# The second layer's input product made in two: values by token, queries and keys pair by pair and already turned

## The chip, the cores and the metric

The kernel runs on one core of a Trainium2 chip, as one launch. The metric is the device time of a launch in microseconds. Its engines are TensorE (PE: matmuls and turns, with PEld for the weight loads), VectorE (DVE), ScalarE (ACT), GpSimd (POOL) and SyncE (SP, which here only issues loads and the final stores); 16 DMA engines carry the transfers.

## What is computed

256 tokens of width 1,024 in float32 go through a two-layer transformer and then a third, wider block. What matters here is the mixer of the second layer:

```python
CD_SPLITS = (FOX_HEADS * HEAD_DIM,) * 3 + (FOX_HEADS,) + (CK_HEADS * HEAD_DIM,) * 3
CD_MIX = (FOX_HEADS + CK_HEADS) * HEAD_DIM
...
def _mixer_cd(h, w_in, b_forget, rel_bias, w_out):
    B, S, _ = h.shape
    proj = jnp.einsum('bsd,df->bsf', h, w_in)
    q_f, k_f, v_f, f_logit, q_c, k_c, v_c = _split_cols(proj, CD_SPLITS)
    o_c = _forgetting_attention(q_f.reshape(B, S, FOX_HEADS, HEAD_DIM), k_f.reshape(B, S, FOX_HEADS, HEAD_DIM),
                                v_f.reshape(B, S, FOX_HEADS, HEAD_DIM), f_logit, b_forget)
    o_d = _chunk_relpos_attention(q_c.reshape(B, S, CK_HEADS, HEAD_DIM), k_c.reshape(B, S, CK_HEADS, HEAD_DIM),
                                  v_c.reshape(B, S, CK_HEADS, HEAD_DIM), rel_bias)
    o = jnp.concatenate([o_c.reshape(B, S, -1), o_d.reshape(B, S, -1)], -1)
    return jnp.einsum('bsf,fd->bsd', o, w_out)
```

Both attentions have 8 heads of width 64. Their logits get a table added (a decay that depends on `f_logit`, or a bias by distance), then softmax, then the product with the values. `w_in` has 3,080 columns: 8 forget logits and 16 heads x (query, key, value) x 64.

## The kernel before

Weights come in chunks of up to 128 x 1,024: SyncE loads a chunk into one of four `stage` buffers (`load_chunk`), ScalarE casts it to the high half (`split_hi`, L1022), VectorE subtracts to get the low half (`split_lo`, L1326), and TensorE uses both. Four pairs of halves (`base_hi`, `base_lo`) go round, and four more (`extra_...`) at the changes between layers. The semaphores `staged`, `hi_done`, `lo_done` and `chunk_used` carry this chain; a stage buffer is free when its chunk's low half is made.

**A product by token** (`gemm`, `step`). The weights' columns are cut into steps; a step sums over 8 blocks of 128 rows. For each block and each of two token tiles of 128, the activations (`xt_hi`, `xt_lo`: turned, 128 rows of width by 256 tokens) are what is loaded into the array, and the weights stream through it: L564 (high, high), L566 (high, low), L569 (low, high). The sums, 128 tokens x n columns, lie in one of two pairs of PSUM banks; ScalarE copies them out at the end of a step (L1173). The second layer's input product `cd_in` has 7 steps of 440 columns in 28 chunks of 2 row blocks; its first two steps are written in another order (`first_steps`: L701, L705, L711), since the token tiles come one after the other from the first layer's last norm. There the turned activations come from L536 (four turns of 128 x 128), ScalarE's cast L1057 and VectorE's L1366.

**Attention, beside the products.** Two heads are a pair; the second layer has pairs 8 to 15. Each pair goes through four places in the stream of chunks, listed by hand in `STAGES`: (turn, logits, turned probabilities, sums). A place is the moment after a chunk; place 0 to 27 are `cd_in`'s chunks, then those of the output product `cd_out`. On TensorE, `turn_pair` (L840) turns two tiles of queries and two of keys, `multiply_pair` (L856) makes the logits, `turn_probs` (L870) turns the probabilities and `sum_pair` (L887) multiplies them with the values. Between them VectorE copies the turned tiles to `qk_t` (L1446), adds the table and takes maxima (L1462, L1473), ScalarE takes exponentials (L1117), VectorE scales (L1485), ScalarE copies the turned probabilities (L1125) and casts the sums (L1130), VectorE makes their low half (L1491). All engines work in the order of their program, so a wait holds up what stands behind it.

**Around it.** `cd_out` (L612) uses the pairs' sums as activations; its last four row blocks are taken half by half (the tail), and pair 15's sum stands inside the tail (`in_tail`). Before `cd_in`, in the order of VectorE's program, stand the splits of its first four chunks and then the norm of the first layer's end: sum (L1540), statistics (L1520), and the normalised halves of a token tile (L1552, L1557), for which TensorE's turns (L536) wait.

## Time and profile before

| | us |
|---|---|
| median of 3 runs (935.96 to 936.83) | 936.23 |
| the profiled execution | 934.53 |
| its span | 932.8 |
| TensorE busy | 917.3 (98%) |
| VectorE busy | 582.2 (62%) |
| ScalarE busy | 481.7 (52%) |
| GpSimd busy | 33.3 (4%) |
| granted clock of TensorE, mean | 0.999 of 2.4 GHz |

Times in the rows are counted from the start of the span. A row of the timeline gives the start, the duration, and in brackets how long the engine was idle before and what released it. Matmuls overlap in the array, so that what one costs is read from the distance between two starts, not from its duration.

### The profile page before, as it was taken

What the parts mean: (1) busy time and instruction counts of PE and PEld (TensorE: products, weight loads), DVE (VectorE), ACT (ScalarE), POOL (GpSimd) and SP (SyncE); (2) the same over time, 40 slices, a digit from 0 to 9 for tenths busy, and PEclk for the clock granted to TensorE, in tenths of its full rate; (3) what the DMA queues carried; (4) which work ended last, traced back from release to release, by engine and by line L of the source; (5) the groups of instructions that cost most, each with busy time, mean ns of one, the idle gap of its engine ahead of it and who ended that gap; (6) DMA issues with size and microseconds to landing.
All of it is one profiled execution on the core that took longest, in us unless ns stands there. A gap on an engine that the chain in (4) does not pass through costs nothing.

```text
span 932.8 us, 12124 instructions
## 1 busy us (share of the span) xinstructions
PE 917.3 (98%) x4502; PEld 759.5 (81%) x4502; DVE 582.2 (62%) x960; ACT 481.7 (52%) x781; POOL 33.3 (4%) x48
## 2 busy tenths in 40 slices
PE   6999999999999999999999999999999999999997
PEld 5888878888888888887888888878888888888875
DVE  4787687555553856668755555376646666574665
ACT  4876564444442446666444444355455654644443
POOL 1100034000000001000000000000000000000000
PEclk9999999999999999999999999999999999999999
DMA  8654457755564456454755556454554465355551
GB/s 304 242 197 136 147 181 230 265 181 182 180 220 149 147 186 209 130 162 154 259 191 191 185 185 201 147 194 137 195 192 143 147 203 158 113 196 181 200 170 66
DMA packets 46760, 169.20 MB, mean 181 GB/s; under 512 B 5384, under 2 KB 5536, under 8 KB 46064
## 3 DMA queue, kind: packets, MB, share of 16 engines
q1 hardware_dynamic: 44064, 156.09, 50.5%
q0 software_dynamic: 2640, 12.35, 4.1%
q8 instruction: 37, 0.61, 0.3%
q14 instruction: 19, 0.16, 0.0%
HBM read 167.36 MB, written 1.06 MB: 181 GB/s over the span
## 4 chain that ended last, share of the span: by engine, by line
PE 93%; DVE 3%; ACT 2%; DMA 1%; issue 0%; DVEq 0%; SPq 0%; ACTq 0%
PE psum L612 19%; PE psum L564 18%; PE psum L569 18%; PE psum L566 18%; PE psum L701 3%; PE psum L705 3%; PE psum L711 3%; PE psum L856 2%; PE psum L536 2%; PE psum L887 1%; PE psum L870 1%; PE psum L753 1%; DVE base_lo L1326 1%; PE psum L783 1%; PE psum L810 1%; ACT base_hi L1022 1%
## 5 line engine op out<-in xcount | busy, mean ns | idle before, releaser
L1326 DVE TENSOR_TENSOR base_lo<-stage,base_hi 128x1024 fp32r<-128x1024 f32 (+3 forms) x223 | 262.2, 1201 | 101.9 <-ACT base_hi L1022 101.0
L1022 ACT CAST base_hi<-stage 128x1024 fp32r<-128x1024 f32 (+3 forms) x223 | 223.2, 1033 | 56.6 <-PE psum L569 35.5
L564 PE MATMUL psum<-base_hi,xt_hi 128*128 128x512 f32 (+3 forms) x528 | 208.8, 396 | 1.9 <-ACT base_hi L1022 1.6
L566 PE MATMUL psum<-base_lo,xt_hi 128*128 128x512 f32 (+3 forms) x528 | 202.2, 383 | 0.4 <-DVE base_lo L1326 0.4
L569 PE MATMUL psum<-base_hi,xt_lo 128*128 128x512 f32 (+3 forms) x528 | 202.4, 383 | 0.0
L564 PEld LDWEIGHTS psum<-base_hi,xt_hi 128*128 128x128 f32 x528 | 99.7, 189 | 21.9 <-issue 2.8
L569 PEld LDWEIGHTS psum<-base_hi,xt_lo 128*128 128x128 f32 x528 | 99.6, 189 | 18.3 <-DVE xt_lo L1366 0.4
L566 PEld LDWEIGHTS psum<-base_lo,xt_hi 128*128 128x128 f32 x528 | 99.7, 189 | 17.7 <-DVE base_lo L1326 1.1
L1326 DVE TENSOR_TENSOR extra_lo<-stage,extra_hi 128x1024 fp32r<-128x1024 f32 (+1 forms) x68 | 80.8, 1214 | 46.9 <-ACT extra_hi L1022 46.6
L1022 ACT CAST extra_hi<-stage 128x1024 fp32r<-128x1024 f32 (+1 forms) x68 | 69.0, 1045 | 43.4 <-PE psum L612 28.9
L564 PE MATMUL psum<-extra_hi,xt_hi 128*128 128x512 f32 x160 | 63.2, 395 | 0.0
L569 PE MATMUL psum<-extra_hi,xt_lo 128*128 128x512 f32 x160 | 62.4, 390 | 0.0
L566 PE MATMUL psum<-extra_lo,xt_hi 128*128 128x512 f32 x160 | 62.3, 390 | 0.0
L612 PE MATMUL psum<-base_hi,ht_hi 128*128 128x512 f32 x144 | 51.5, 400 | 0.0
L612 PE MATMUL psum<-base_lo,ht_hi 128*128 128x512 f32 x144 | 50.2, 392 | 0.7 <-DVE base_lo L1326 0.7
L612 PE MATMUL psum<-base_hi,ht_lo 128*128 128x512 f32 x144 | 50.1, 391 | 0.0
L1074 ACT CAST ht_hi<-psum 128x512 fp32r<-128x512 f32 x22 | 12.9, 587 | 65.4 <-PE psum L753 65.4
L1187 ACT ACTIVATE qk_t<-psum 128x256 f32<-128x256 f32 x44 | 14.5, 381 | 62.1 <-PE psum L569 54.0
L1373 DVE TENSOR_TENSOR ht_lo<-psum,ht_hi 128x512 fp32r<-128x512 f32 x22 | 15.2, 690 | 49.9 <-ACT ht_hi L1074 49.9
L564 PE MATMUL psum<-base_hi,ht_hi 128*128 128x512 f32 (+1 forms) x106 | 41.2, 389 | 0.0
L569 PE MATMUL psum<-base_hi,ht_lo 128*128 128x512 f32 (+1 forms) x106 | 39.4, 372 | 0.0
L566 PE MATMUL psum<-base_lo,ht_hi 128*128 128x512 f32 (+1 forms) x106 | 39.4, 372 | 0.0
(198 smaller groups left out, 1320.4 us busy)
## 6 DMA issues: line engine op xcount, KB each, us to landing
stage<-in_w_up SPq DMA_DIRECT2D x80, 512.0 KB, 4.4
stage<-in_w_down SPq DMA_DIRECT2D x44, 512.0 KB, 4.3
...
```

Source lines behind the costliest of these rows:

```text
L536: last = pe.transpose(turn_bank(name, g)[:, k * P:(k + 1) * P], src(k0 + k, t), ident[:, :])
L564: pe.matmul(acc, ah, wh, start=(k == 0), stop=False)
L566: pe.matmul(acc, ah, wl, start=False, stop=False)
L569: last = pe.matmul(acc, al, wh, start=False, stop=(k == g.kc - 1))
L612: last = pe.matmul(psum[:, 2 * ((g.u0 + half) % 2) + t, :], a, w(c, half * 512, 512), start=(k == 0 and w is w_hi and a is ah), stop=summed)
L701: pe.matmul(acc, ah, w_hi(c, at, g.n), start=(k == 0), stop=False)
L705: pe.matmul(acc, al, w_hi(c, at, g.n), start=False, stop=False)
L711: last = pe.matmul(acc, ah, w_lo(c, at, g.n), start=False, stop=(k == g.kc - 1))
L856: last = pe.matmul(psum[:, LOGIT_BANK + e, t * P:t * P + nk], qk_t[rows, b, t * P:(t + 1) * P], qk_t[rows, b, S:S + nk], start=True, stop= ...
L1022: act.copy(w_hi(c, 0, w), stage_of(c, w)).then_inc(hi_done, 1)
L1326: dve.tensor_tensor(w_lo(c, 0, w), stage_of(c, w), w_hi(c, 0, w).bitcast(F32), ALU.subtract).then_inc(lo_done, 1)
L1373: dve.tensor_tensor(ht_lo[:, at, :], turn_bank(name, g).rearrange("p (k n) -> p k n", k=2), ht_hi[:, at, :].bitcast(F32), ALU.subtract).th ...
```

## The change

The columns of `cd_in` are the same, and so is what is computed with them. They are now made by two products. `cd_v` makes the forget logits and the values, 1,032 columns, by token as before: 3 steps of 344 columns, 12 chunks of 2 row blocks. `cd_qk` then makes queries and keys in 8 steps, one for each pair. In a step the weights are loaded into the array (128 query columns or 128 key columns of the pair at a time) and the activations stream through it, so that the sums come out turned, channel by token. `xt_hi` and `xt_lo` now lie side by side in one tile `xt`, so that a high-weights matmul of 512 columns makes the products with both halves of all 256 tokens in one bank; a low-weights matmul of 256 columns adds its part to the first 256. At the end of a step ScalarE copies columns 256 to 512 of both banks to `qk_t` (`copy_lows`) and VectorE adds columns 0 to 256 (`add_lows`). The turns `turn_pair` and the copies `copy_pair` of pairs 8 to 15 are gone. A chunk of `cd_qk` has 4 row blocks of 256 columns; there are 16.

The weights lie in memory in blocks of 128 rows with all 3,080 columns, and are picked from there: a chunk of `cd_qk` in one transfer with rows of 1 KB, a chunk of `cd_v` in 3 or 4 transfers (`value_pieces`), where one transfer with rows of 3,520 bytes stood before. The table of places is adapted, and pair 15's sum stands after `cd_out`'s chunk 3.

```diff
-             ("cd_in", 8, 2, 440, 7), ("cd_out", 8, 1, 1024, 1), ("up1", 8, 2, 512, 11), ("down1", 22, 1, 1024, 1),
+             ("cd_v", 8, 2, CD_V // 3, 3), ("cd_qk", 8, 4, 256, 8), ("cd_out", 8, 1, 1024, 1), ("up1", 8, 2, 512, 11), ("down1", 22, 1, 1024, 1),
...
+def pair_block(pair, n):
+    return FOX_H + (3 * pair + n) * 2 * HD
+def value_pieces(step):
+    n = CD_V // 3
+    blocks = [(0, FOX_H, 0)] + [(FOX_H + 2 * HD * p, 2 * HD, pair_block(p, 2)) for p in range((FOX_H + CK_H) // 2)]
+    pieces = []
+    for at, width, column in blocks:
+        lo, hi = max(at, step * n), min(at + width, (step + 1) * n)
+        if lo < hi:
+            pieces.append((lo - step * n, hi - lo, column + lo - at))
+    return pieces
+def loads_of(g, n):
+    return len(value_pieces(n * g.kp // g.kc)) if g.name == "cd_v" else 1
...
-            count[s] = count.get(s, 0) + 1
+            count[s] = count.get(s, 0) + loads_of(g, n)
...
-L1_PLACES = [("cd_in", n) for n in range(28)] + [("cd_out", n) for n in range(5)]
+L1_PLACES = ([("cd_v", n) for n in range(12)] + [("cd_qk", n) for n in range(16)]
+             + [("cd_out", n) for n in range(4)])
...
-    (11, 12, 15, 16), (13, 14, 17, 18), (15, 16, 19, 20), (17, 18, 21, 22), (21, 22, 25, 26), (23, 24, 27, 28),
-    (25, 26, 28, 29), (28, 29, 31, 32)])})
+    (13, 14, 17, 18), (15, 16, 19, 20), (17, 18, 21, 22), (19, 20, 23, 24), (21, 22, 25, 26), (23, 24, 27, 28),
+    (25, 26, 29, 30), (27, 28, 30, 31)])})
...
-        xt_hi = sb("xt_hi", [P, 8, S], F32R)
-        xt_lo = sb("xt_lo", [P, 8, S], F32R)
+        xt = sb("xt", [P, 8, 2, S], F32R)
+        xt_hi, xt_lo = xt[:, :, 0, :], xt[:, :, 1, :]
...
+        def pair_sums(j):
+            u = PRODUCTS["cd_qk"].u0 + j
+            both = psum[:, 2 * (u % 2):2 * (u % 2) + 2, :]
+            return u, qk_t[:, j % 2, :].rearrange("p (b n) -> p b n", b=2), both[:, :, 0:S], both[:, :, S:2 * S]
...
+            def cd_columns(k0, count, column, width):
+                return bass.AP(tensor=d["w_cd_in"].tensor, offset=k0 * P * CD_W + column,
+                               ap=[[CD_W, P], [P * CD_W, count], [1, width]])
             def load_chunk(g, n):
                 c = g.c0 + n
                 if STAGE_LAST[c] >= 0:
                     sp.wait_ge(lo_done, STAGE_LAST[c] + 1)
-                sp.dma_start(stage_of(c, WIDTH[c]), d["w_" + g.name][n]).then_inc(staged[STAGE[c]], 16)
-            for g in GEMMS.values():
+                if g.name == "cd_qk":
+                    sp.dma_start(stage_of(c, WIDTH[c]).rearrange("p (k n) -> p k n", k=g.kp),
+                                 cd_columns(n % 2 * g.kp, g.kp, pair_block(n // 2, 0), g.n)
+                                 ).then_inc(staged[STAGE[c]], 16)
+                elif g.name == "cd_v":
+                    for at, width, column in value_pieces(n * g.kp // g.kc):
+                        sp.dma_start(stage_of(c, WIDTH[c]).rearrange("p (k n) -> p k n", k=g.kp)[:, :, at:at + width],
+                                     cd_columns(n * g.kp % g.kc, g.kp, column, width)).then_inc(staged[STAGE[c]], 16)
+                else:
+                    sp.dma_start(stage_of(c, WIDTH[c]), d["w_" + g.name][n]).then_inc(staged[STAGE[c]], 16)
...
-                                if in_tail and t == 0 and halves[0] == 0 and k == end - 3:
-                                    in_tail()
...
-                pe.wait_ge(pair_copied, p + 1)
+                if p < 8:
+                    pe.wait_ge(pair_copied, p + 1)
+                else:
+                    pe.wait_ge(*read("cd_qk", p - 7))
...
-                    turn_pair(p)
+                    if p < 8:
+                        turn_pair(p)
...
-            first_steps("cd_in", "x1", 1, {7: lambda: [heads_banks("f1"), cumulate()]})
-            gemm("cd_in", xt_hi, xt_lo, 0, None, attending("cd_in", *range(8, 28)), first=2)
+            def step_by_pair(j):
+                g = PRODUCTS["cd_qk"]
+                u = g.u0 + j
+                pe.wait_ge(acc_free[u % 2], 2 * (u // 2))
+                for m in range(2):
+                    c = g.c0 + 2 * j + m
+                    for kk in range(g.kp):
+                        k = m * g.kp + kk
+                        for high in ((True, False) if k < g.kc - 1 else (False, True)):
+                            for b in range(2):
+                                acc, at = psum[:, 2 * (u % 2) + b, :], kk * g.n + b * P
+                                if high:
+                                    pe.wait_ge(hi_done, c + 1)
+                                    last = pe.matmul(acc, w_hi(c, at, P), xt[:, k, :, :].rearrange("p a n -> p (a n)"),
+                                                     start=(k == 0), stop=(k == g.kc - 1))
+                                else:
+                                    pe.wait_ge(lo_done, c + 1)
+                                    last = pe.matmul(acc[:, 0:S], w_lo(c, at, P), xt_hi[:, k, :],
+                                                     start=False, stop=False)
+                    last.then_inc(chunk_used, 1)
+                    attend("cd_qk", 2 * j + m)
+            first_steps("cd_v", "x1", 1, {7: lambda: [heads_banks("f1"), cumulate()]})
+            gemm("cd_v", xt_hi, xt_lo, first=2)
+            for j in range(8):
+                step_by_pair(j)
             wide("cd_out", ht_hi, ht_lo, None, between=attending("cd_out", *range(4)), first_turn=first_part("f1", 2),
-                 first_pair=8, in_tail=lambda: attend("cd_out", 4))
+                 first_pair=8)
...
+            def copy_lows(j):
+                u, dst, highs, lows = pair_sums(j)
+                act.wait_ge(chunk_used, PRODUCTS["cd_qk"].c0 + 2 * j + 2)
+                act.wait_ge(pair_logits, max(8, 8 + j - 1))
+                act.copy(dst, lows).then_inc(pair_lows, 1)
+            gemm("cd_v", copy_to(lambda j, t, acc: (proj1[:, t, j * 344:(j + 1) * 344], acc[:, 0:344])),
+                 {4: log_sigmoid})
+            gemm("cd_qk", None, {**attending("cd_qk", *range(16)),
+                                 **{2 * j + 1: lambda j=j: [copy_lows(j), attend("cd_qk", 2 * j + 1)]
+                                    for j in range(8)}})
+            wide("cd_out", attending("cd_out", *range(4)), TAIL)
...
+            def add_lows(j):
+                u, dst, highs, lows = pair_sums(j)
+                dve.wait_ge(pair_lows, j + 1)
+                dve.tensor_tensor(dst, dst, highs, ALU.add).then_inc(acc_free[u % 2], TT)
+            gemm("cd_v", None, {4: forget_abs, 5: forget_log, 7: copy_cumulated})
+            gemm("cd_qk", None, {**attending("cd_qk", *range(16)),
+                                 **{2 * j + 1: lambda j=j: [add_lows(j), attend("cd_qk", 2 * j + 1)]
+                                    for j in range(8)}})
+            wide("cd_out", attending("cd_out", *range(4)), 2)
```

In the order of TensorE's program, at a turn (L840) between two chunks of `cd_in` before:

```order
L564 MATMUL psum<-base_hi,xt_hi 128x440 [waits hi_done]
L566 MATMUL psum<-base_lo,xt_hi 128x440 [waits lo_done]
L569 MATMUL psum<-base_hi,xt_lo 128x440
L840 MATMUL psum<-ident,arena 128x128 [waits pair_copied,acc_free0]
L840 MATMUL psum<-ident,arena 128x128 x3
L564 MATMUL psum<-base_hi,xt_hi 128x440 [waits hi_done]
L566 MATMUL psum<-base_lo,xt_hi 128x440 [waits lo_done]
L569 MATMUL psum<-base_hi,xt_lo 128x440
L564 MATMUL psum<-base_hi,xt_hi 128x440 [waits hi_done]
```

and in the new program, in the middle of a step of `cd_qk` (L1009 and L1013 are `step_by_pair`, L924 is `sum_pair`, L893 is `multiply_pair`, "xt" the activations):

```order
L1009 MATMUL psum<-xt,base_hi 128x512 [waits hi_done] x2
L1013 MATMUL psum<-xt,base_lo 128x256 [waits lo_done] x2
L924 MATMUL psum<-probs_t,arena 64x256 [waits pair_copied,acc_free1,o_lo,probs_copied]
L924 MATMUL psum<-probs_t,arena 64x256
L924 MATMUL psum<-probs_t,arena 64x128 x2
L893 MATMUL psum<-qk_t 128x128 [waits probs_copied,pair_max,acc_free1]
L893 MATMUL psum<-qk_t 128x128
L893 MATMUL psum<-qk_t 128x256 x2
L1009 MATMUL psum<-xt,base_hi 128x512 [waits hi_done] x2
L1013 MATMUL psum<-xt,base_lo 128x256 [waits lo_done] x2
L1009 MATMUL psum<-xt,base_hi 128x512 [waits hi_done] x2
```

No turn stands there any longer; the logits wait for the accumulator's semaphore `acc_free`, which VectorE's add raises, in place of `pair_copied`.

In the order of ScalarE's program, around the end of a step with a pair's exponentials, before (L1117 exponentials, L1173 copies of the sums, L1125 turned probabilities, L1022 high halves):

```order
L1022 CAST base_hi<-stage 128x880 [waits chunk_used,staged0]
L1117 ACTIVATE pair_probs,pair_st<-pair_probs,pair_st 128x128 [waits pair_max]
L1117 ACTIVATE pair_probs,pair_st<-pair_probs,pair_st 128x256
L1117 ACTIVATE pair_probs,pair_st<-pair_probs,pair_st 128x128
L1117 ACTIVATE pair_probs,pair_st<-pair_probs,pair_st 128x256
L1173 COPY arena<-psum 128x440 [waits chunk_used]
L1173 COPY arena<-psum 128x440
L1125 COPY probs_t<-psum 128x2x384 [waits pair_summed,probs_turned]
L1022 CAST base_hi<-stage 128x880 [waits chunk_used,staged1]
```

and in the new program (L1183, L1311, L1191 and L1088 are the same four):

```order
L1183 ACTIVATE pair_probs,pair_st<-pair_probs,pair_st 128x128 [waits pair_max]
L1183 ACTIVATE pair_probs,pair_st<-pair_probs,pair_st 128x256
L1183 ACTIVATE pair_probs,pair_st<-pair_probs,pair_st 128x128
L1183 ACTIVATE pair_probs,pair_st<-pair_probs,pair_st 128x256
L1311 COPY qk_t<-psum 128x512 [waits pair_logits,chunk_used]
L1191 COPY probs_t<-psum 128x2x384 [waits pair_summed,probs_turned]
L1088 CAST base_hi<-stage 128x1024 [waits chunk_used,staged1]
```

One copy of 128 x 512 stands where two of 128 x 440 stood, behind the exponentials again, and the logits of the step's pair now depend on it.

In the order of SyncE's program, the loads before:

```order
L422 DMA late_stage_50<-in_w_up 128x1024 x2
L422 DMA stage<-in_w_up 128x1024 [waits lo_done] x40
L422 DMA stage<-in_w_down 128x1024 [waits lo_done] x22
L422 DMA stage<-in_w_cd_in 128x880 [waits lo_done] x28
L422 DMA stage<-in_w_cd_out 128x1024 [waits lo_done] x8
L422 DMA late_stage_49<-in_w_up 128x1024 [waits lo_done,pair_max,chunk_used]
```

and in the new program, up to the second chunk of `cd_v`:

```order
L463 DMA stage<-in_w_down 128x1024 [waits lo_done] x22
L460 DMA stage<-in_w_cd_in 128x2x8 [waits lo_done]
L460 DMA stage<-in_w_cd_in 128x2x128 x2
L460 DMA stage<-in_w_cd_in 128x2x80
L460 DMA stage<-in_w_cd_in 128x2x8 [waits lo_done]
L460 DMA stage<-in_w_cd_in 128x2x128 x2
L460 DMA stage<-in_w_cd_in 128x2x80
L460 DMA stage<-in_w_cd_in 128x2x8 [waits lo_done]
```

A wait for the stage buffer stands ahead of four issues instead of one.

## Rows read from the trace of the kernel before

**Rows 1.** The page: busy time of TensorE; the two halves of the weight split

```profile
PE 917.3 (98%) x4502; PEld 759.5 (81%) x4502; DVE 582.2 (62%) x960; ACT 481.7 (52%) x781; POOL 33.3 (4%) x48
...
L1326 DVE TENSOR_TENSOR base_lo<-stage,base_hi 128x1024 fp32r<-128x1024 f32 (+3 forms) x223 | 262.2, 1201 | 101.9 <-ACT base_hi L1022 101.0
...
L1022 ACT CAST base_hi<-stage 128x1024 fp32r<-128x1024 f32 (+3 forms) x223 | 223.2, 1033 | 56.6 <-PE psum L569 35.5
```

**Rows 2.** Stretches: length, busy PE, PEld, DVE, ACT, POOL, clock, DMA share, GB/s

```profile
339.86:407.41 67.55, 67.55 (x406) 57.42 (x405) 44.87 (x127) 40.84 (x96) 4.98 (x8) 1.00 0.56 178
...
407.41:437.16 29.75, 29.10 (x156) 22.12 (x153) 21.86 (x43) 17.98 (x31) 0.00 (x0) 1.00 0.58 195
```

**Rows 3.** Who waited for whom: TensorE, 296 to 450 us

```profile
PE psum L612 <- DVE base_lo L1326: 0.7, 2, 0.5
```

**Rows 4.** Timeline, TensorE, 440 columns, with a turn: start, duration (us)

```profile
341.13 0.36 PE L566 MATMUL psum<-base_lo,xt_hi 128*128 128x440 f32 x1
...
350.33 0.36 PE L569 MATMUL psum<-base_hi,xt_lo 128*128 128x440 f32 x1
...
350.53 0.60 PE L840 MATMUL psum<-ident,arena 128*128 128x128 f32 x4
...
351.16 0.36 PE L566 MATMUL psum<-base_lo,xt_hi 128*128 128x440 f32 x1
```

**Rows 5.** Timeline, TensorE, at 256 and at 512 columns

```profile
49.24 0.28 PE L564 MATMUL psum<-base_hi,ht_hi 128*128 128x256 f32 x1
...
50.91 0.28 PE L569 MATMUL psum<-base_hi,ht_lo 128*128 128x256 f32 x1
...
428.11 0.40 PE L612 MATMUL psum<-base_hi,ht_hi 128*128 128x512 f32 x1
...
434.74 0.39 PE L612 MATMUL psum<-base_hi,ht_lo 128*128 128x512 f32 x1
```

**Rows 6.** Timeline, ScalarE: turned tile; a pair's last exponential

```profile
327.50 0.59 ACT L1057 CAST xt_hi<-psum 128x512 fp32r<-128x512 f32 x1 [3.57 <-PE psum L536]
...
371.27 0.49 ACT L1117 ACTIVATE pair_probs<-pair_probs,pair_st 128x256 f32<-128x256 f32 x1
```

**Rows 7.** Timeline, VectorE, at the first layer's last norm

```profile
310.28 1.08 DVE L1326 TENSOR_TENSOR extra_lo<-stage,extra_hi 128x880 fp32r<-128x880 f32 x1 [0.71 <-ACT extra_hi L1022]
...
313.57 0.69 DVE L1540 SCALAR_TENSOR_TENSOR x<-x,psum 128x512 f32<-128x512 f32 x1 [0.89 <-PE psum L612]
...
316.25 0.75 DVE L1557 SCALAR_TENSOR_TENSOR x<-x,ln_st,ln_par 128x512 f32<-128x512 f32 x1
...
325.68 0.75 DVE L1557 SCALAR_TENSOR_TENSOR x<-x,ln_st,ln_par 128x512 f32<-128x512 f32 x1
...
328.12 0.69 DVE L1366 TENSOR_TENSOR xt_lo<-psum,xt_hi 128x512 fp32r<-128x512 f32 x1 [1.69 <-ACT xt_hi L1057]
```

**Rows 8.** Timeline, TensorE: turns after the norm; a pair's sum and logits

```profile
317.38 0.60 PE L536 MATMUL psum<-ident,x 128*128 128x128 f32 x4
...
326.87 0.60 PE L536 MATMUL psum<-ident,x 128*128 128x128 f32 x4
...
328.09 0.60 PE L536 MATMUL psum<-ident,x 128*128 128x128 f32 x4
...
366.68 0.87 PE L887 MATMUL psum<-probs_t,arena 128*64 128x256 f32 x8
...
367.48 0.93 PE L856 MATMUL psum<-qk_t 64*128 64x128 f32 x8
```

**Rows 9.** Timeline, SyncE's queue: issues of transfers

```profile
1.24 0.42 SPq L416 DMA_DIRECT2D ident<-in_ident  x1
...
1.71 0.90 SPq L422 DMA_DIRECT2D stage<-in_w_ab_in  x2
...
300.69 0.33 SPq L422 DMA_DIRECT2D stage<-in_w_cd_in  x1
```

**Rows 10.** SyncE's issue line, 298 to 350 us

```profile
DMA to landing us min/median/max: 3.1/4.5/6.9
```

90 lines of the change are left out of this document (39 added, 51 removed).

## Prediction, on record before the changed kernel was run

> **What bounds the kernel now.** I read the page first: TensorE is busy for 98% of the span and carries 93% of the chain that ended last [rows 1]. The other engines matter only where they make TensorE wait or hand it more work. The view by stretches then says the same of the part that is changed: in the input product of the second layer (339.9 to 407.4 us) TensorE is busy for 67.55 of 67.55 us, at a granted clock of 1.00 (2.4 GHz), with the 16 DMA engines at 56%; only in the output product after it is 0.65 us missing [rows 2]. The list of waits agrees: from 296 to 450 us TensorE waited 0.7 us in all, for two low halves of weights in the tail of that output product [rows 3]. So a microsecond taken from TensorE's stream there is a microsecond of the result, unless a new wait eats it, and no waiting can be won but that 0.7 us.
>
> "Busy" hides what one matmul costs, since the bars overlap (a bar of 0.36 us, while starts are 0.20 us apart). I therefore work with the spacing of starts. At 440 columns there are 46 spacings between the starts at 341.13 and 350.33 us: 0.200 us each [rows 4]. At 256 columns 14 spacings lie between 49.24 and 50.91 us: 0.119 us. At 512 columns 29 lie between 428.11 and 434.74 us: 0.2286 us [rows 5]. Each of these matmuls loads its own weights, and the load does not show beyond this spacing, not even at 256 columns.
>
> **The change, part by part.** *The product's own matmuls.* Before: 7 steps x 8 row blocks x 2 token tiles x 3 passes = 336 of 440 columns, 147,840 columns. After: values 3 x 8 x 2 x 3 = 144 of 344 columns; queries and keys 8 steps x 8 x 2 = 128 of 512 and 128 of 256 columns: again 147,840. In time: before 336 x 0.200 = 67.2 us. For 344 columns I interpolate between 256 and 440: 0.119 + 88/184 x 0.081 = 0.158 us. After: 144 x 0.158 + 128 x 0.2286 + 128 x 0.119 = 22.7 + 29.3 + 15.3 = 67.3 us. **+0.1 us**, for 64 matmuls more.
>
> The Trainium skill speaks against this on the page "TensorE: Matmul & The Clock Gate", section "Back-to-back issue gap": in a stream of weight loads and matmuls it gives 131 ns at N=512 and 81 ns at N=128, so most of the cost belongs to the matmul and little to its columns. Drawn as a line, an estimate from that page is 122 ns at 440, 109 at 344 and 98 at 256 columns: 41.0 us before, 45.0 after, +4.0 us in place of +0.1. The measured 228.6 ns at 512 columns disagree with it, and the rows decide.
>
> *The turns of queries and keys.* Eight times TensorE turned two query and two key tiles of a pair (L840, x4). A turn costs the stream more than its start shows: the last matmul ahead of it starts at 350.33, the second behind it at 351.16, 0.83 us where two spacings are 0.40 [rows 4]. 8 x 0.43 = **-3.4 us**. What depended on them, the 0.69 us copies on VectorE, ran beside the product and gives TensorE nothing. The attention inserts themselves (logits, turned probabilities, sums) are as many as before; two of them stand together once more than they did, which saves one restart of the stream of about 0.1 us (0.28 instead of 0.20 us behind an insert, [rows 4]): **-0.1 us**.
>
> *The new link between product and logits.* Before, logits waited for one VectorE copy, issued a place ahead. Now, when a pair's step ends, ScalarE copies the low sums and VectorE adds the high ones; the logits wait for that. No such pair of instructions is in the trace; by the nearest 128x512 rows it is 0.59 us (ScalarE from PSUM) and 0.69 us (VectorE from PSUM) [rows 6, 7]. ScalarE has the previous pair's exponentials ahead of it. Logits that start at 367.48 [rows 8] have their last exponential starting at 371.27, done at 371.76 [rows 6]: 4.3 us after. In the new order the step ends 0.86 us (the logits matmuls, taken from their bar of 0.93) + one chunk of 8 x 0.2286 + 8 x 0.119 = 2.8 us after the same point, so 3.65 us: ScalarE is 0.65 us late (367.48 + 4.28 against 367.48 + 3.65), the sum is there 0.65 + 0.59 + 0.69 + 0.2 for two hand-overs = 2.1 us after the step. TensorE asks for it after the turned probabilities, another chunk (2.8) and the earlier pair's sum (0.8: its start at 366.68, the logits' at 367.48): 3.6 us without the probabilities. At least 1.5 us to spare, eight times: **0**. Bounds: 0 if the spare time holds; if each engine had its longest neighbour, a split of 1.0 and 1.2 us [rows 1], in front of it once more, 0.7 us per pair is missing, less the time of the six turned probabilities (0.4 us or more): 0.3 us, 2.4 us in all. Only at the end is it tighter: the output product's second accumulator needs the last pair's sum (2.1 us) after 6 x 0.2286 = 1.4 us and those probabilities: **+0.1**.
>
> *The entry from the first layer.* Before the second token tile's turns TensorE now has narrower work. Up to the first turn it does 36 matmuls, up to the second 40; at 0.042 us less each it arrives 1.5 and 1.7 us sooner, at 325.4 instead of 326.87 and at 326.4 instead of 328.09 [rows 8]. The norm's last write on VectorE runs from 325.68 to 326.43 [rows 7]. What was 1.7 us of cover becomes zero: I take **+0.2 us**, between 0 and 0.8.
>
> *The loads.* A values chunk comes in 3 or 4 pieces with rows of 32 to 512 bytes, where one issue with rows of 3,520 bytes stood; 44 issues for 12 chunks. A piece of 256 short rows on SyncE's queue is not in the trace. Issues there follow each other every 0.47 us (1.24 to 1.71) [rows 9], and the quickest whole chunk of 440 KB was there 3.1 us after its issue [rows 10]; a last piece of 80 KB needs no more than that, and I take 2.3 us. VectorE splits the first four of these chunks before it starts the norm of the first layer's end: before, the fourth split started at 310.28, and the norm later waited 0.89 us for TensorE until 313.57 [rows 7]. After: 16 issues from 300.69 (first row of [rows 9]), the last at 300.69 + 15 x 0.47 = 307.7, landed 310.0, cast 0.7, split 0.85: 311.6. The norm's first half (0.68 + 0.69 and the steps between, 1.4 us) ends at 313.0, before TensorE's half. **0**, with 0.5 us to spare, and 0.38 us more behind it (the norm's write ends at 317.00, TensorE's turn starts at 317.38 [rows 7, 8]). The bound above is a rival below. The pair chunks are one issue of 512 rows of 1 KB and have some 4 us of TensorE's time each: 0.
>
> *The end of the output product.* The last pair's sum now stands at a chunk's end and not inside the tail, so ScalarE is held back from the last splits less long. The 0.7 us of [rows 3] lie here, in two waits with a restart of 0.1 us each: 0.9 us. After, the last low half still comes late: ScalarE's cast of the sum (0.4 us, estimated from 0.59 for twice the width), hi split 1.0 and lo split 1.2 [rows 1], with 0.3 us of hand-overs 2.9 us after the sum, when TensorE wants it after 10 spacings of 0.2286, 2.3 us: 0.6 us, with a restart 0.7. **-0.2 us**, between 0 and -0.9.
>
> Sum: +0.1 - 3.4 - 0.1 + 0.1 + 0.2 - 0.2 = **-3.3 us**. The span is 932.8 us and the profiled execution 934.53 us with the 1.7 us around it, so 931.2; the median of the three runs is 936.23, 1.7 us above the profiled one, so **932.9 us**.
>
> **The rivals.**
> *The pieces come late.* At a pitch p between issues the fourth chunk's split ends at 311.6 + 15 (p - 0.47). From p = 0.53 TensorE waits, and each further 0.1 us costs 1.5 us; 0.6 costs 1.1 us (934.0), 0.7 costs 2.6 (935.5), 0.9 costs 5.6 (938.5, slower). A piece that lands 2 us later instead costs 1.1 us. For it: three times the issues of a shape not in the trace. Against: the pitch is that of any transfer shown, and the data need less than the DMA engines' idle half. 19%. The Trainium skill's page "DMA: Bandwidth & Descriptors", section "Specifications", has 512 B as the least transfer at line rate and says that shorter ones are read, modified and written; 20 of the 44 pieces are shorter. No row here shows it; it would make this rival likelier, which is counted in the 19%.
>
> *New waits in the pair chain or at the entry.* 0.3 us at each logits (2.4) or 0.8 at the entry: 933.7 to 935.3. For it: two engines in place of one, and no cover left at the entry. Against: the 1.5 us to spare. 11%.
>
> *The stream of alternating widths is slower (the other side).* If the weight load (0.188 us as a bar) does not fit behind a 256-column matmul when it is followed by another load, the 128 low matmuls are 0.188 instead of 0.119 us apart: +8.8 us, 941.7, slower. It decides at 26 ns per low matmul (gain gone). Against: the 256-column stretch has a load with every matmul and keeps 0.119. 5%, the page's 4 us included.
>
> *More than forecast*, if the whole tail stall goes and nothing new comes, 4.2 us in place of 3.3: 932.0 or less, 3%. The forecast itself 62%.
>
> **Numbers.** 0.2%, 1.9 us, is about what a measurement of this kernel tells from no change: faster below 934.4, slower above 938.1. The forecast's own range is 932.0 to 934.0. Faster: 62 + 3 + half of the second rival + a quarter of the first, about 71%. Same: the rest of both and the weaker end of the third, 19%. Slower: 10%. The range that leaves out 2 in 10 goes up over half of the first rival and down past the best sum: 931.5 to 936.6.
>
> **What would show it.** Right: the stretch from the first product matmul to the output product shorter by about 3.4 us beyond the entry; starts 0.229 and 0.119 us apart in the new stream; no wait of TensorE on the new VectorE add; SyncE's issues 0.47 us apart; the first layer's norm starting at the same time. Wrong: a wait for the norm's write at the first turn, a longer pitch of issues, low matmuls further apart than 0.13 us, or TensorE held at the logits by the add.

## The result, and the profile after

| | before | changed |
|---|---|---|
| median of its runs | 936.1 us (934.46 to 936.83, 4 runs) | 929.97 us (929.34 to 931.11, 4 runs) |
| ratio | | 0.9942, 95% interval 0.993 to 0.9954 |
| profiled execution, its span | 934.53, 932.8 us | 930.03, 928.3 us |

By the medians the changed kernel is 6.1 us faster, by the ratio 5.4 us (4.3 to 6.6), where 3.3 were forecast. Its time lies 1.5 us below the forecast's wider range (931.5 to 936.6 us), in the part that was given 3%. The direction and the main mechanism (the turns leave TensorE's stream) were right. One term was mis-sized, and so was the level on which the sum was set, as the rows show.

The page, and the two stretches that answer to [rows 2] (the product of values, queries and keys from its third step on; the output product with the next norm's first turns). The first of them can't be set against before's as it stands, since it holds 2,392 of the 3,080 columns here and 2,200 there; the table further down compares like with like.

```profile
PE 913.2 (98%) x4534; PEld 755.9 (81%) x4534; DVE 582.1 (63%) x960; ACT 482.5 (52%) x781; POOL 34.4 (4%) x48
```

```profile
337.39:404.66 67.27, 67.27 (x437) 56.56 (x436) 45.98 (x127) 42.85 (x97) 5.97 (x8) 1.00 0.66 197
404.66:432.75 28.09, 27.94 (x148) 21.33 (x147) 21.42 (x42) 17.34 (x28) 0.00 (x0) 1.00 0.60 207
```

TensorE is again busy all the time at a granted clock of 1.00 (2.4 GHz), and 4.1 us less of it is needed. Its waits from 296 to 450 us, against 0.7 us in [rows 3]:

```profile
PE psum L653 <- DVE base_lo L1401: 0.2, 1, 0.2
```

The timeline of TensorE in the new stream: L607 and L610 are two of the three passes at 344 columns, L1009 the 512-column matmul of queries and keys (two to a row), L1013 the 256-column one.

```profile
337.39 0.31 PE L607 MATMUL psum<-base_lo,xt 128*128 128x344 f32 x1
...
344.63 0.32 PE L610 MATMUL psum<-base_hi,xt 128*128 128x344 f32 x1
344.79 0.63 PE L1009 MATMUL psum<-xt,base_hi 128*128 128x512 f32 x2
345.26 0.40 PE L1013 MATMUL psum<-xt,base_lo 128*128 128x256 f32 x2
345.49 0.63 PE L1009 MATMUL psum<-xt,base_hi 128*128 128x512 f32 x2
```

46 spacings from 337.39 to 344.63 us are 0.157 us each; two 512-column matmuls take 0.47 us and two 256-column ones 0.23 us, 0.70 together. The forecast had 0.158 us for the first, and 2 x 0.2286 + 2 x 0.119 = 0.695 us for the others.

**Where the time went**, by starts of TensorE that both timelines have (A: second turn of the first layer's last norm, B: first matmul of the output product, C: first turn of the norm after it, D: first turn of the norm after the feed-forward, E: its last turn):

| stretch | before | after | difference | forecast |
|---|---|---|---|---|
| start to A | 319.21 | 319.57 | +0.36 | 0 |
| A to B | 88.20 | 85.09 | -3.11 | -2.8 |
| B to C | 27.56 | 26.26 | -1.30 | -0.5 |
| C to D | 187.30 | 186.94 | -0.36 | 0 |
| D to E | 12.28 | 12.20 | -0.08 | 0 |
| E to the end | 298.25 | 298.24 | 0 | 0 |

The forecast column is its own sum laid out by place. Seven of the eight turns stood between A and B, the eighth in the output product, so of -3.4 a share of -3.0 goes to A to B and -0.4 to B to C. From A to E the profiled executions differ by 4.85 us, not 3.3; about half of what is missing lies in B to C. (The second pair of profiles, runs 1 and 12, differs by 4.60: 315.05 and 310.45 us.) The +0.36 ahead of A has nothing to do with the change: 0.34 of it is there at the first layer's first norm, whose turns start at 130.45 us before and at 130.79 after.

### The profile page after: what moved, and what is told of

Same layout as the page of the kernel before. It is cut to its first block, busy times and chain, and to the rows that moved or that the text cites. A ratio compares the mean times of both kernels' runs of the same rounds, so it can differ in the third digit from the quotient of the medians.

```text
span 928.3 us, 12232 instructions
## 1 busy us (share of the span) xinstructions
PE 913.2 (98%) x4534; PEld 755.9 (81%) x4534; DVE 582.1 (63%) x960; ACT 482.5 (52%) x781; POOL 34.4 (4%) x48
## 4 chain that ended last, share of the span: by engine, by line
PE 96%; DVE 2%; ACT 2%; DMA 1%; issue 0%; SPq 0%; DVEq 0%; ACTq 0%
PE psum L653 21%; PE psum L605 17%; PE psum L610 17%; PE psum L607 17%; PE psum L1009 3%; PE psum L740 3%; PE psum L744 3%; PE psum L750 3%; PE psum L893 2%; PE psum L1013 2%; PE psum L577 1%; PE psum L924 1%; PE psum L907 1%; PE psum L792 1%; PE psum L822 1%; PE psum L849 1%
## 5 line engine op out<-in xcount | busy, mean ns | idle before, releaser
L1088 ACT CAST base_hi<-stage 128x1024 fp32r<-128x1024 f32 (+3 forms) x223 | 224.4, 1036 | 58.1 <-PE psum L610 32.7
L605 PE MATMUL psum<-base_hi,xt 128*128 128x512 f32 (+3 forms) x464 | 183.5, 395 | 2.6 <-ACT base_hi L1088 2.3
L607 PE MATMUL psum<-base_lo,xt 128*128 128x512 f32 (+3 forms) x464 | 178.3, 384 | 0.4 <-DVE base_lo L1401 0.4
L610 PE MATMUL psum<-base_hi,xt 128*128 128x512 f32 (+3 forms) x464 | 178.6, 385 | 0.0
L605 PEld LDWEIGHTS psum<-base_hi,xt 128*128 128x128 f32 x464 | 87.7, 189 | 19.4 <-ACT base_hi L1088 2.7
L610 PEld LDWEIGHTS psum<-base_hi,xt 128*128 128x128 f32 x464 | 87.6, 189 | 17.2 <-DVE xt L1441 0.4
L607 PEld LDWEIGHTS psum<-base_lo,xt 128*128 128x128 f32 x464 | 87.7, 189 | 17.1 <-DVE base_lo L1401 1.1
L1088 ACT CAST extra_hi<-stage 128x1024 fp32r<-128x1024 f32 (+1 forms) x68 | 68.4, 1037 | 47.4 <-PE psum L653 26.4
L605 PE MATMUL psum<-extra_hi,xt 128*128 128x512 f32 x160 | 63.2, 395 | 0.0
L610 PE MATMUL psum<-extra_hi,xt 128*128 128x512 f32 x160 | 62.4, 390 | 0.0
L607 PE MATMUL psum<-extra_lo,xt 128*128 128x512 f32 x160 | 62.4, 390 | 0.0
L1009 PE MATMUL psum<-xt,base_hi 128*128 128x512 f32 x128 | 41.0, 404 | 0.0
L610 PE MATMUL psum<-base_hi,ht_lo 128*128 128x512 f32 (+1 forms) x106 | 39.4, 372 | 0.0
```

The costliest lines, as they stand in the source:

```text
L605: pe.matmul(acc, ah, wh, start=(k == 0), stop=False)
L607: pe.matmul(acc, ah, wl, start=False, stop=False)
L610: last = pe.matmul(acc, al, wh, start=False, stop=(k == g.kc - 1))
L1009: last = pe.matmul(acc, w_hi(c, at, P), xt[:, k, :, :].rearrange("p a n -> p (a n)"), start=(k == 0), stop=(k == g.kc - 1))
L1088: act.copy(w_hi(c, 0, w), stage_of(c, w)).then_inc(hi_done, 1)
```

## The experiments

Times are medians. Each group ran on one chip beside its own runs of before: 935.36 us (17 runs) for the first four, 935.64 (21) for the next four, 935.66 (21) for the last four.

**1. The changed kernel again.**

> The changed kernel itself once more, on the chip of the runs beside it. Theory A (the parts add up: turns 3.4 us, the tail of the output product 0.9, the entry and the link 0, so some 4.5 to 4.9 us as in the two profiled executions): ratio 0.9950, gain 4.3 to 5.0 us. Theory B (timed executions of the kernel before carry a loss of 1 to 2 us that its profiled one does not show and that the change removes): gain 5.8 to 6.5 us, ratio 0.9935.

Measured: 930.48 us (929.80 to 930.63, 5 runs), ratio 0.9939 (0.9927 to 0.9951); profiled 930.58. With the four runs above, nine executions of the changed kernel have their median at 930.26 us. Seventeen more of before gave 935.36. By these medians the gain is 4.9 us; by the ratio it is 5.7 (4.6 to 6.8), so this run by itself does not tell theory A from theory B. All executions together give 935.65 - 930.26 = 5.4 us (run 12).

**2. Before, without the turns of pairs 8 to 15.**

```diff
             def attend(name, n):
...
-                    turn_pair(p)
+                    if p < 8:
+                        turn_pair(p)
...
-                    copy_pair(p)
+                    if p < 8:
+                        copy_pair(p)
```

> The kernel before with one part of the change alone: the eight turns of queries and keys and their copies on VectorE are left out, and the logits of pairs 8 to 15 are made from stale tiles. If a turn costs TensorE's stream 0.43 us and nothing else hangs on it: 3.4 us faster, within 0.3. Rival: the copies on VectorE or the wait for the copy held TensorE up unseen as well: 4.5 us or more faster. A third possibility, that the stream only moves its waits (the tail stays as it is): 2.5 us or less.

Measured: 933.05 us (932.01 to 935.02, 7 runs), ratio 0.9971 (0.996 to 0.9983), 2.3 us faster than before by the medians and 2.7 by the ratio. The profile says why it is not 3.4: with the turns gone, TensorE comes to pair 8's probabilities before VectorE has masked pair 9, and VectorE had waited for the decay table that GpSimd builds for pairs 8 to 11 (VectorE's and TensorE's timeline; in brackets the idle time ahead and who ended it):

```profile
356.55 0.29 DVE L1464 CUSTOM_DVE_ANT_0 pair_probs<-psum,fox_table 128x128 f32<-128x128 f32 x1 [2.83 <-POOL fox_table L504]
```

```profile
363.25 0.17 DVE L1475 TENSOR_SCALAR pair_st<-pair_st 128x4 f32<-128x4 f32 x1
```

```profile
363.52 0.84 PE L871 MATMUL psum<-ident,pair_probs 128*128 128x128 f32 x6 [1.02 <-issue]
```

The profile names no releaser for the wait of 1.02 us, but in the program TensorE waits there for pair 9's maxima, whose last instruction (L1475) ends at 363.42 us, 0.1 ahead. In the trace A to C is 2.2 us shorter than in before, and with the wait and a restart of 0.1 us that makes the turns' 3.3. The tail's two waits are still there (0.6 us), so the third possibility has the size nearly right, but for another reason. The turns alone could not have been removed from before at their full price: pair 9's maxima end at 362.42 us there and TensorE comes at 363.09, which is some 0.6 us to spare, and in this run the table came 0.9 us later by itself (13.6 us behind the store in place of 12.7).

**3. The changed kernel with eight idle turns.**

```diff
                 for p in at_stage((name, n), 0):
                     if p < 8:
                         turn_pair(p)
+                    else:
+                        for m in range(4):
+                            pe.transpose(psum[:, QK_BANK, m * P:(m + 1) * P], x[:, m % 2, m * P:(m + 1) * P],
+                                         ident[:, :])
```

> The changed kernel with eight idle turns (four transposes of 128x128 each, of other data, results unused) at the places where a pair's turn would stand. Theory: 8 x 0.43 = 3.4 us slower than the changed kernel. What is then left against the kernel before is the gain of everything but the turns: by theory A 1.2 us, by theory B 2.5 us or more.

Measured: 934.16 us (933.11 to 935.06, 10 runs), 3.7 us above run 1 on the same chip. In its trace A to B is 88.68 us, 3.59 more than after: 0.45 us for each turn, against 0.43 in the forecast. The rest of the change, without the turns' gain, is worth 1.2 us against before by the medians, 1.7 (0.8 to 2.5) by the ratio.

**4. The changed kernel with the last pair's sum back inside the tail.**

```diff
-    (25, 26, 29, 30), (27, 28, 30, 31)])})
+    (25, 26, 29, 30), (27, 28, 31, 32)])})
...
+                                if in_tail and t == 0 and halves[0] == 0 and k == end - 3:
+                                    in_tail()
```

> The changed kernel with the last pair's turned probabilities and sum put back where they stood before: the probabilities after chunk 3 of the output product, the sum inside its tail. Theory: the tail's loss comes back, TensorE waits twice for low halves there: 0.9 us slower than the changed kernel (between 0.7 and 1.2), and nothing else moves. Rival (my forecast's size for this part): 0.2 us slower.

Measured: 931.37 us (930.80 to 931.40, 5 runs), 0.9 us above run 1. B to C is 27.21 us, 0.95 more than after, with the two waits of [rows 3] back (0.6 us in all). So the place of that sum is worth 0.9 us, which the forecast had at 0.2.

**5. The kernel before without the wait for the decay table.**

```diff
-                return Head(HD, HD ** -0.5, q, k, v, fox_table[:, h, :], False, cut(o1, h * HD, HD), None, None)
+                return Head(HD, HD ** -0.5, q, k, v, table[:, h, :], False, cut(o1, h * HD, HD), None, None)
...
-                if p == 8 or p == 10:
-                    dve.wait_ge(fox_masked, 2 if p == 8 else 4)
+                if p == 8:
+                    dve.wait_ge(rel_ready, 2)
                 if p == 12:
-                    dve.wait_ge(rel_ready, 2)
+                    dve.wait_ge(fox_masked, 4)
```

> The kernel before, with one thing changed in the computation: the scores of pairs 8 to 11 get the relative-position table added in place of the decay table, so that VectorE no longer waits for GpSimd's decay table before it masks pair 8. Every instruction stays in its place; only that wait is gone. In the profiled execution of before the masking of pair 8 waits 1.95 us for the table and TensorE's copies of pair 8's probabilities then come through with some 0.6 us to spare; in the run without turns the same chain was 1.0 us late. Theory A (in many timed executions of before the table comes later still, and TensorE waits for pair 8): the median falls by 0.5 to 1.5 us against the kernel before and the spread of the executions, 3.2 us so far, shrinks to about 1.5 us. Theory B (the spread of before has another source, such as start-up or the first layer): no change within 0.3 us and the same spread.

Measured: 935.23 us (934.29 to 936.94, 11 runs), ratio 0.9994 (0.9985 to 1.0003). The spread of before is still there (2.6 us against 2.3), so the table is not its main source. The median moved by 0.4 us, inside an interval of -1.4 to +0.3: whether late tables cost the timed executions some tenths isn't decided by it.

**6 and 7. The changed kernel with a later decay table.** The change makes the values first, so the table's chain starts 3.6 us earlier (GpSimd stores its rows at 338.08 us, before at 341.63). These two runs take that back and more: the store comes 5.3 us later than in after in the first and 6.2 us in the second.

```diff
                 pool.wait_ge(cum_copied, 1)
+                pool.wait_ge(hi_done, PRODUCTS["cd_qk"].c0 + 1)
                 pool.dma_start(fox_rows, cum_k[0:FOX_H, :]).then_inc(fox_stored, 16)
```

(`+ 2` in the other.)

> The changed kernel; GpSimd stores the cumulated decay only after the high halves of the first chunk of queries and keys are written, some 4 us later than it does there and about when the kernel before does. Nothing else moves. The chain from that store to the table took 12.7 to 14.0 us in six profiles, so the table comes at about 356 us in place of 352, the masking of pair 8 ends at about 358.5, and that of pair 9, which must end before TensorE copies pair 8's probabilities at 363.6, at 363.5 to 365. Theory A (that chain is a part of the gain): 0.3 to 1.3 us slower than the changed kernel (930.5 us on the first chip), with a wait of TensorE at pair 8's probabilities in the profile and a wider spread. Theory B (the chain has time to spare in both kernels): no change within 0.3 us.

> As the run before it, with the store after the second chunk of queries and keys, some 5.9 us later than in the changed kernel. Theory A: TensorE waits 2 to 3 us at pair 8's probabilities, and the time is 2 to 3 us above the changed kernel's, that is 932.5 to 933.5 us; each further us of delay costs about a whole one. Theory B: no change, or under 0.5 us.

Measured: 931.13 us (930.65 to 931.64, 5 runs) and 934.75 us (931.84 to 937.53, 11 runs): 0.9 and 4.5 us above the nine runs of the changed kernel, which ran on other chips. Theory A's size holds for the first run and is too small for the second, and the place was wrong in both: TensorE did not wait at pair 8's probabilities but at pair 9's logits (0.5 and 3.1 us). VectorE and TensorE of the later one:

```profile
358.05 0.29 DVE L1538 CUSTOM_DVE_ANT_0 pair_probs<-psum,fox_table 128x128 f32<-128x128 f32 x1 [5.07 <-POOL fox_table L546]
```

```profile
362.66 0.93 PE L894 MATMUL psum<-qk_t 64*128 64x128 f32 x8 [3.11 <-DVE qk_t L1774]
```

The masking waits 5.07 us, pair 8's exponentials on ScalarE wait for the masking, ScalarE's copy of pair 9's low sums stands behind the exponentials in its queue, and the adding step behind the copy. So what makes one pair late makes the next pair's link late as well.

The wait is not all that the later run lost. A to B is 89.86 us, 4.77 more than in after: 3.2 lie ahead of pair 9's logits, and 1.6 behind them, where no wait is listed. There, behind the idle stretch of 3.11 us, TensorE's granted clock had fallen from 2.4 to 1.2 GHz, from 364.1 to 367.5 us. The last number but two of this row is the clock of a stretch, as a share of 2.4 GHz:

```profile
364.00:367.00 3.00, 3.00 (x12) 2.55 (x11) 2.96 (x11) 0.78 (x3) 0.00 (x0) 0.51 0.73 204
```

The timed executions fit that: the two whose mean clock was 0.999 took 931.84 and 933.10 us, the nine at 0.995 to 0.997 took 933.50 to 937.53. In the first run, with its wait of 0.5 us, the clock stayed at 1.00.

**8. A longer link between product and logits.**

```diff
+                for _ in range(3):
+                    settle(dve.tensor_copy(row_g[:, 0:512].rearrange("p (b n) -> p b n", b=2), highs))
```

> The changed kernel with three idle copies of 128x512 on VectorE ahead of each pair's adding step, each finished before the next, some 2.2 us more in the link between a pair's queries and keys and its scores, eight times. In the profile after, that add ends 2.45 us before TensorE comes to the scores of that pair. Theory A (the link is hidden with about 2.4 us to spare, as the forecast had it at no cost): no change within 0.5 us. Rival (some pairs have less to spare, or VectorE's splits of weights come late behind the longer link): a wait of 0.3 us or more for each pair, 2 us or more in all.

Measured: 944.69 us (944.02 to 944.82, 4 runs), 14 us more. I had counted spare time in the wrong place. The forecast's link in the profile after (ScalarE, VectorE, TensorE):

```profile
371.77 0.50 ACT L1183 ACTIVATE pair_probs<-pair_probs,pair_st 128x256 f32<-128x256 f32 x1
...
372.26 0.57 ACT L1311 COPY qk_t<-psum 128x512 f32<-128x512 f32 x1
```

```profile
372.93 0.69 DVE L1773 TENSOR_TENSOR qk_t<-qk_t,psum 128x512 f32<-128x512 f32 x1 [1.35 <-ACT qk_t L1311]
```

```profile
376.07 0.93 PE L893 MATMUL psum<-qk_t 64*128 64x128 f32 x8
```

The add ends at 373.62, TensorE comes at 376.07: 2.45 us to spare for this pair (2.3 to 2.6 for six of the eight, 1.3 and 1.0 for the first two). But logits, masking, exponentials, copy, add and the next pair's logits form a ring. With the three copies it takes 9.25 us from logits to logits:

```profile
371.39 0.93 PE L893 MATMUL psum<-qk_t 64*128 64x128 f32 x8 [0.75 <-DVE qk_t L1775]
```

```profile
380.64 0.93 PE L893 MATMUL psum<-qk_t 64*128 64x128 f32 x8 [0.86 <-DVE qk_t L1775]
```

Less the 2.14 us of the copies and some 0.1 us between them that is 7.0 us, where the stream gives it 8.09 (376.07 to 384.16). The ring has 1.1 us to spare, not 2.45: VectorE's scaling and its split stand behind the add, and the next masking behind them.

The ring is only a part of the 14 us. In the trace A to B is 93.00 us, 7.9 more than in after: those are the ring's losses. B to C is 32.22 us, 5.96 more. Of these, 3.07 us are one wait of the output product's second accumulator for the last pair's add, and the clock takes most of the rest. It was at 1.2 GHz from 416.6 to 423.4 us, after seven waits of up to 1.2 us and inside this last one:

```profile
417.62 0.80 PE L653 MATMUL psum<-base_hi,ht_hi 128*128 128x512 f32 x1 [3.07 <-DVE qk_t L1775]
```

```profile
417.00:423.00 6.00, 5.38 (x22) 3.53 (x22) 3.21 (x8) 0.93 (x2) 0.00 (x0) 0.50 0.31 89
```

From that matmul to the first one behind the logits (423.50) it takes 5.89 us, where the same instructions take 3.12 in after: 2.8 us for the clock.

**9. Each chunk of values loaded by one issue.**

```diff
-    return len(value_pieces(n * g.kp // g.kc)) if g.name == "cd_v" else 1
+    return 1
...
+    weights["cd_v"] = np.concatenate([cd[:, :FOX_H]] + [cd[:, pair_block(p, 2):pair_block(p, 2) + 2 * HD]
+                                                        for p in range(8)], 1)
```

> The changed kernel with the columns of the values laid out one behind the other in memory, so that each of their 12 chunks is loaded by one issue in place of 3 or 4. The computation is the same. In the profile after, the pieces are issued every 0.47 us and land in a median of 2.5 us, and TensorE does not wait for the first layer's norm that stands behind them on VectorE. Theory A (the pieces cost nothing, as forecast): no change within 0.4 us of the changed kernel. Rival (pieces with rows of 32 to 512 bytes slow other transfers, or move the norm at the entry): 0.5 to 1.5 us faster.

Measured: 930.94 us (929.78 to 931.22, 5 runs); the nine runs of the changed kernel have 930.26. That is 0.7 us more, just outside theory A's 0.4 but on the side away from the rival's gain, and against other chips; in the traces nothing differs (A to B 85.11 us, B to C 26.26, after 85.09 and 26.26). So the pieces cost the time nothing, as forecast. They do hold up the norm at the entry a little, as the rival had it: without them its write ends 0.37 us ahead of TensorE's first turn (317.07 and 317.44), with them 0.1 (317.64 and 317.73). Their group in the profile after (the first three numbers are the duration of an issue in ns), and the first 16 issues on SyncE's queue:

```profile
L460 SPq DMA_DIRECT2D stage<-in_w_cd_in x44: 368/469/1115, 301.1 to 335.8; - x44
...
DMA to landing us min/median/max: 2.0/2.5/3.8
```

```profile
301.06 8.06 SPq L460 DMA_DIRECT2D stage<-in_w_cd_in  x16
```

An issue lasts 0.469 us, but the next one starts 0.51 us after it: 8.06 us for 16, less the last one's 0.47, over 15. The forecast and the expectation above have 0.47 us as the distance.

**10. The changed kernel, last free split ahead of the last sum.**

```diff
                 if (name, n) in LAST_SUMS:
-                    split_to(min(done["due"], PRODUCTS[LAST_SUMS[name, n]].c0))
+                    end = PRODUCTS[LAST_SUMS[name, n]].c0
+                    split_to(min(ahead(end - 4), end))
```

(on ScalarE and on VectorE)

> The changed kernel; ScalarE and VectorE split the last free chunk of the output product's weights before they take up the last pair's sum, not behind it. In the profile after, the one wait for that chunk reads 0.15 us, but the starts around it (0.55 us in place of 0.23, then 0.34 in place of 0.24) make it cost 0.42 us. Theory A (a listed wait costs its length and about 0.3 us of restart): 0.4 us faster than the changed kernel, at the edge of what can be told, and no wait left in the output product. Theory B (the cost of a wait is its listed length): 0.15 us, no difference. Rival: the last sum now comes late and its own split is waited for, 0 to 0.7 us slower.

Measured: 929.08 us (928.86 to 929.69, 5 runs), ratio 0.9928 (0.9915 to 0.9942) against before, 1.2 us under the nine runs of the changed kernel on other chips and 1.9 under run 9 on the same one. Of that the trace shows 0.48: B to C is 25.78 us in place of 26.26, and TensorE has no wait from 296 to 640 us. This is the fastest version measured here.

**11. The kernel before, one split ahead of the copy of the last probabilities.**

```diff
                 for p in at_stage((name, n), 2):
+                    if p == PAIRS - 1:
+                        split_to(done["chunks"] + 1)
                     copy_probs(p)
```

> The kernel before; ScalarE splits one chunk of the output product's weights before it copies the last pair's turned probabilities, not behind that copy (it had been idle for 2.06 us there). Nothing else changes. In the profile of before the two waits for the next chunks read 0.5 and 0.2 us, while the starts around them show 1.29 us lost. Theory A (that stall is the tail's term and costs 1.3 us, of which the change saved 0.9): 0.8 to 1.3 us faster than the kernel before. Theory B (a stall costs its listed length): 0.5 to 0.7 us. Rival (the tail has nothing to do with it and the gain beyond the turns comes from the earlier layer): no change.

Measured: 933.78 us (933.17 to 936.51, 11 runs), 1.9 us under before by the medians; ratio 0.9985 (0.9976 to 0.9994), 1.4 us (0.6 to 2.2). B to C is 26.60 us in place of 27.56, 0.96 less. Theory A's 0.8 to 1.3 us is met by the trace, and by the ratio within its interval. The timeline of the tail in before, where the sum stands just ahead of the first row, and in this run:

```profile
425.32 0.50 PE L612 MATMUL psum<-base_hi,ht_hi 128*128 128x512 f32 x1
426.30 0.50 PE L612 MATMUL psum<-base_lo,ht_hi 128*128 128x512 f32 x1 [0.48 <-DVE base_lo L1326]
426.64 0.40 PE L612 MATMUL psum<-base_hi,ht_lo 128*128 128x512 f32 x1
...
427.44 0.51 PE L612 MATMUL psum<-base_lo,ht_hi 128*128 128x512 f32 x1 [0.17 <-DVE base_lo L1326]
427.78 0.49 PE L612 MATMUL psum<-base_hi,ht_lo 128*128 128x512 f32 x1
428.11 0.40 PE L612 MATMUL psum<-base_hi,ht_hi 128*128 128x512 f32 x1
```

```profile
425.69 0.50 PE L612 MATMUL psum<-base_hi,ht_hi 128*128 128x512 f32 x1
426.03 0.39 PE L612 MATMUL psum<-base_lo,ht_hi 128*128 128x512 f32 x1
...
427.35 0.39 PE L612 MATMUL psum<-base_hi,ht_hi 128*128 128x512 f32 x1
```

Six spacings behind the sum take 2.79 us in before and 1.66 here. So waits of 0.65 us in the list cost 1.1 us and more. ScalarE's idle time was there, 2.06 us ahead of its copy of the last turned probabilities:

```profile
423.24 0.80 ACT L1125 COPY probs_t<-psum 128x768 f32<-128x768 f32 x1 [2.06 <-PE psum L870]
```

**12. The kernel before again.**

> The kernel before, unchanged, for a second profiled execution of it and for the spread of its timed ones. The forecast put the changed kernel's timed executions 1.7 us above its profiled one because before's median of three was. Theory A (that distance was a draw: the three were high and the profiled one was low): the median lies at 935.2 to 935.8 us, and the new profiled execution may fall anywhere between 934.3 and 937 us. Theory B (a profiled execution is by its nature 1 to 2 us quicker than timed ones): the new profiled one is again at about 934.5 us, with timed ones near 936.

Measured: 935.45 us (934.48 to 936.18, 11 runs), profiled 935.52. Theory A holds. Of the other 63 timed executions of the kernel before in this study the median is 935.65 us (934.31 to 937.56), and only four were as quick as the one profiled at first. The two profiled executions of before differ by 1.28 us at the turn of 317.38 us [rows 8], and 0.87 of it is there at an early turn of TensorE (first the earlier profile, then this run's):

```profile
12.12 0.60 PE L566 MATMUL psum<-base_lo,xt_hi 128*128 128x480 f32 x1
12.52 0.44 PE L569 MATMUL psum<-base_hi,xt_lo 128*128 128x480 f32 x1
12.80 0.38 PE L564 MATMUL psum<-base_hi,xt_hi 128*128 128x480 f32 x1
...
16.07 1.04 PE L536 MATMUL psum<-ident,x 128*128 128x128 f32 x8
```

```profile
14.34 0.58 PE L566 MATMUL psum<-base_lo,xt_hi 128*128 128x480 f32 x1
14.74 0.40 PE L569 MATMUL psum<-base_hi,xt_lo 128*128 128x480 f32 x1
14.98 0.38 PE L564 MATMUL psum<-base_hi,xt_hi 128*128 128x480 f32 x1
...
16.94 1.03 PE L536 MATMUL psum<-ident,x 128*128 128x128 f32 x8
```

The first matmuls of the program, of 480 columns, start 0.40 us apart, and then 0.22: up to 12.5 us in the one profile, up to 14.7 in the other. Those are five or six more at the slow spacing, some 1.0 us, and less the 0.2 us by which the second execution was ahead until then (12.34 against 12.52) they are the 0.87. (The column of the granted clock reads 1.00 in both at that place, so only the spacings tell it.) From there to the output product both take the same time within 0.4 us. That part of the spread lies ahead of everything that was changed.

## Why the prediction was right, and where it failed

- **The stream of the product, +0.1.** Right: spacings of 0.157, 0.235 and 0.115 us. The Trainium skill's page "TensorE: Matmul & The Clock Gate", section "Back-to-back issue gap", from whose figures the forecast estimated 4 us more for the narrower matmuls, was rightly set aside: its 131 ns at N=512 are 0.23 us here, and A to B became shorter by what the turns took.
- **The turns, -3.4.** Right: -3.6 by run 3 (0.45 us each), -3.3 by run 2.
- **The link, 0, and +0.1 at the end.** Right for this kernel: no wait in eight pairs. Its margin of "at least 1.5 us" was too kind: 1.0 us at pair 9, and 1.1 us in the ring that runs through all pairs (run 8).
- **The entry, +0.2.** Nothing of it came. The norm's last write on VectorE ends at 326.54 us and TensorE turns its tile from 326.87 without a wait: of the 1.7 us of cover [rows 7, 8] 0.3 are left, where the forecast saw none.

```profile
325.79 0.75 DVE L1633 SCALAR_TENSOR_TENSOR x<-x,ln_st,ln_par 128x512 f32<-128x512 f32 x1
```

```profile
326.87 0.60 PE L577 MATMUL psum<-ident,x 128*128 128x128 f32 x4
```

- **The loads in pieces, 0.** Right as to the time: run 9 gains nothing without them. The pitch was not: issues start 0.51 us apart, not 0.47, and land after 2.5 us against the 2.3 taken. In this execution the queue also began 0.36 us later, as everything there did. So the fourth chunk's split ends at 312.85 us, not at 311.6, and the norm's first half is done at 314.2 and not at 313.0. The spare time of 0.5 us was spent, and 0.3 of the 0.38 behind it: the norm's second sum starts at 314.21 us where it started at 313.57 [rows 7], now without a wait for TensorE, and its write ends at 317.64, 0.1 us ahead of the turn at 317.73. That it cost nothing was in part luck.

```profile
311.98 0.88 DVE L1401 TENSOR_TENSOR extra_lo<-stage,extra_hi 128x688 fp32r<-128x688 f32 x1 [1.21 <-ACT extra_hi L1088]
...
314.21 0.69 DVE L1616 SCALAR_TENSOR_TENSOR x<-x,psum 128x512 f32<-128x512 f32 x1
```

  The Trainium skill's page "DMA: Bandwidth & Descriptors" ("Specifications": transfers under 512 B are below line rate, since they are read, modified and written) would have made them dearer. No cost of it can be seen in the time.
- **The end of the output product, -0.2: this term was mis-sized.** It measured -0.85 in the trace and 0.9 us in run 4. The step took the two waits at 0.7 us and a restart of 0.1 each, 0.9, and then left 0.7 standing in the changed kernel. The starts around the waits say 1.28 us for before (six spacings behind the sum in 2.79 us, run 11, where the same six take 1.51 in after), and 0.44 for after (1.13 us from 422.94 to 424.07, where three spacings are 0.69):

```profile
420.73 0.50 PE L653 MATMUL psum<-base_hi,ht_hi 128*128 128x512 f32 x1
421.07 0.40 PE L653 MATMUL psum<-base_lo,ht_hi 128*128 128x512 f32 x1
...
422.24 0.39 PE L653 MATMUL psum<-base_hi,ht_hi 128*128 128x512 f32 x1
...
422.94 0.40 PE L653 MATMUL psum<-base_hi,ht_hi 128*128 128x512 f32 x1
423.49 0.50 PE L653 MATMUL psum<-base_lo,ht_hi 128*128 128x512 f32 x1 [0.15 <-DVE base_lo L1401]
423.83 0.40 PE L653 MATMUL psum<-base_hi,ht_lo 128*128 128x512 f32 x1
424.07 0.40 PE L653 MATMUL psum<-base_hi,ht_hi 128*128 128x512 f32 x1
```

  The rows were there: spacings, which the prediction used for the turns, would have given the 1.3, and ScalarE's 2.06 us of idle time ahead of the copy of the probabilities (run 11) says that the splits came late only by their place in the queue.
- **The level: "the median of the three runs is 936.23, 1.7 us above the profiled one, so 932.9".** This step failed outright, and against the best median of before there is, it put the forecast 0.55 us too high. The 1.7 us are no property of a profiled execution but two draws, a quick profile and three slow runs. The changed kernel's two profiled executions (930.03, 930.58) sit on its median of 930.26. Set on the median of 63 runs of before, the same sum gives 935.65 - 3.3 = 932.35, and with the tail as it measured 931.7. That is still 1.4 us above the measured 930.26. Of these some 0.9 are in the traces: the entry and the last link, which cost nothing (0.3), turns at 0.45 us (0.2) and C to D (0.36). The rest is open.
- **The chances.** By the forecast's own rule "faster" adds up to 62 + 3 + 5.5 + 4.75 = 75%, not to about 71. And the side on which the result fell was given 3%, though the tail's waits could be had from spacings.
- **What stays open.** 935.65 - 930.26 is 5.4 us; the traces have 4.85 from A to E (4.60 in the second pair), of which 0.36 lie in C to D, unforecast: there TensorE waited for a norm's write in before (0.2 us listed). The stretch is 186.93 to 186.95 us in all nine profiles of the changed kernel and its variants, but 187.30, 187.07, 187.15, 187.43 and 186.90 in the five of before and its variants. So a gain of about 0.2 us is usual there, and the 0.36 partly chance; why before needs longer was not tried. Why the timed executions differ by 0.5 us more was not settled; the decay table could be part of it, since the changed kernel starts its chain 3.6 us earlier and runs 6 and 7 show that it loses time when the table is late, but run 5 moved the median by only 0.4 us, within its interval. For it speaks run 11's profile: the table came 13.3 us behind the store there, pair 9's maxima ended at 363.34 us and TensorE's turn started at 363.44, so of before's 0.6 us to spare nothing was left. Nor was it tried why the timed executions of run 10 gained 0.7 us more than its B to C; for run 11 the medians say 0.9 more, the ratio 0.4.
